# Attention stage of a hybrid decoder layer: three PSUM banks in turn for transposed probabilities, four for scores, with scores issued three tiles ahead instead of four

## What is computed

```python
s_win = jnp.einsum('bhqd,bkd->bhqk', qb, k_win).astype(f32) * scale
p_win = jax.nn.softmax(jnp.where(m_win, s_win, NEG_INF), axis=-1).astype(v_win.dtype)
o_win = jnp.einsum('bhqk,bkd->bhqd', p_win, v_win)
```

## Time and profile before

| | |
|---|---|
| median of three runs | 603.61 us (603.17 to 603.81) |
| the profiled execution | 603.88 us, of which the span is 602.1 us |
| PE busy | 590.5 us (98% of the span) |
| DVE busy | 390.1 us (65%) |
| ACT busy | 300.0 us (50%) |
| POOL busy | 257.0 us (43%) |
| attention loop | about 156.7 to 210 us of the span |
| granted TensorE clock | 0.997 of full speed |

### The profile page before, as it was taken

How to read it: one execution, slowest core, us unless ns; L and a number is a source line. 1 busy time by engine, 2 the same in 40 slices (tenths; PEclk the granted TensorE clock), 3 DMA queues, 4 the chain that set the end, 5 groups by cost and what they waited for, 6 DMA issues and landing times.

```text
span 602.1 us, 8286 instructions
## 1 busy us (share of the span) xinstructions
PE 590.5 (98%) x3095; PEld 484.5 (80%) x3095; DVE 390.1 (65%) x666; ACT 300.0 (50%) x529; POOL 257.0 (43%) x138
## 2 busy tenths in 40 slices
PE   8999999999999999999999999999999999999995
PEld 5898888877866678899878888888888888888884
DVE  6414605266978774983999777585595685771656
ACT  6713414654589934555645545444355265354322
POOL 7763323573094610043357443631723626611611
PEclk9999999999999999999999999999999999999998
DMA  8743282466023710028034340621603404104002
GB/s 326 288 144 137 72 208 71 87 161 208 1 45 104 264 63 0 1 72 280 1 143 137 136 144 1 209 71 67 202 12 139 141 0 153 57 1 175 1 35 106
DMA packets 36580, 67.18 MB, mean 112 GB/s; under 512 B 2876, under 2 KB 23612, under 8 KB 35516
## 3 DMA queue, kind: packets, MB, share of 16 engines
q1 hardware_dynamic: 36236, 66.25, 34.0%
q10 hardware_dynamic: 304, 0.39, 0.3%
HBM read 62.18 MB, written 2.10 MB: 107 GB/s over the span
## 4 chain that ended last, share of the span: by engine, by line
PE 89%; ACT 4%; DVE 3%; issue 2%; DMA 1%; SPq 0%; POOLq 0%; POOL 0%; ACTq 0%; DVEq 0%
PE ps L1814 19%; PE ps L1816 19%; PE ps L1815 19%; PE ps L2288 7%; PE ps L2290 7%; PE ps L2289 7%; PE ps L2140 2%; PE ps L2155 2%; PE ps L2051 1%; PE ps L2052 1%; ACT probs L949 1%; DMA x_land<-in_x_turned 1%; ACT W L890 1%; PE ps L1979 1%; PE ps L2216 1%
## 5 line engine op out<-in xcount | busy, mean ns | idle before, releaser
L1814 PE MATMUL ps<-xT_h,ring_h 128*128 128x512 f32 (+1 forms) x384 | 144.3, 376 | 0.3 <-DVE q_far L1361 0.3
L1816 PE MATMUL ps<-xT_h,ring_l 128*128 128x512 f32 (+1 forms) x384 | 143.2, 373 | 0.0
L1815 PE MATMUL ps<-xT_l,ring_h 128*128 128x512 f32 (+1 forms) x384 | 143.1, 373 | 0.0
L773 POOL TENSOR_TENSOR ring_l<-raw_d,ring_h 128x1024 fp32r<-128x1024 f32 x25 | 67.3, 2699 | 129.8 <-ACT ring_h L1044 129.8
L773 POOL TENSOR_TENSOR ring_l<-raw,ring_h 128x1024 fp32r<-128x1024 f32 x31 | 76.7, 2499 | 77.5 <-DVE xres L1630 38.1
L692 POOL TENSOR_TENSOR ring_l<-raw,ring_h 128x512 fp32r<-128x512 f32 (+2 forms) x26 | 64.2, 2489 | 74.1 <-ACT ring_h L796 74.1
L1724 DVE TENSOR_TENSOR y<-ps,y 128x512 f32<-128x512 f32 x90 | 61.2, 689 | 50.9 <-PE ps L2290 50.6
L1814 PEld LDWEIGHTS ps<-xT_h,ring_h 128*128 128x128 f32 x384 | 72.4, 188 | 14.0 <-issue 1.3
L1816 PEld LDWEIGHTS ps<-xT_h,ring_l 128*128 128x128 f32 x384 | 72.3, 188 | 12.9
L1815 PEld LDWEIGHTS ps<-xT_l,ring_h 128*128 128x128 f32 x384 | 72.4, 189 | 12.5
L2288 PE MATMUL ps<-ring_h,a_h 128*128 128x512 f32 x196 | 76.7, 391 | 0.1
(11 more groups left out here) (276 smaller groups left out, 994.7 us busy)
## 6 DMA issues: line engine op xcount, KB each, us to landing
raw<-in_w_mlp SPq DMA_DIRECT2D x16, 1024.0 KB, 5.6
raw_d<-in_w_mlp SPq DMA_DIRECT2D x16, 1024.0 KB, 6.1
raw<-in_w_groups SPq DMA_DIRECT2D x8, 1024.0 KB, 4.8
xres<-in_x SPq DMA_DIRECT2D x8, 512.0 KB, 6.3
raw<-in_nsa_cmp_w SPq DMA_DIRECT2D x8, 512.0 KB, 6.6
raw<-in_w_groups SPq DMA_DIRECT2D x8, 256.0 KB, 5.5
raw<-in_w_out SPq DMA_DIRECT2D x2, 1024.0 KB, 6.2
raw<-in_w_out SPq DMA_DIRECT2D x4, 512.0 KB, 4.8
```

Of the source, the lines that this page charges most:

```text
L773: nc.gpsimd.tensor_tensor(slot(ring_l, n), slot_source(n), slot(ring_h, n).bitcast(F32), ALU.subtract).then_inc(lo_done, 1)
L1814: nc.tensor.matmul(o, sh, mh, start=start, stop=False)
L1815: nc.tensor.matmul(o, sh, ml, start=False, stop=False)
L1816: return nc.tensor.matmul(o, sl, mh, start=False, stop=stop)
```

## The change

Scores get four banks instead of five, and transposed probabilities three instead of two. The banks of the transposed probabilities are no longer tied to the head but taken in turn. So `transposes(s)` waits for the copy of tile s - 3 instead of s - 2 (a copy that the other engine makes), and `score(s)` waits for the exponential of tile s - 4 instead of s - 5. In PE's loop iteration s issues `score(s + 3)` instead of `score(s + 4)`; the waits for `cs_sub` and for `reads(J_MK[1])` move into iterations 0 and 2. On DVE `copy_t(u)` is ahead of `row_max(2u + 4)`. Behind the loop `y_transposes(2)` comes after `values(5)` and waits for `attn_out(4)`; it has bank 6 instead of 3.

```diff
-S_BANK = [2, 3, 7, 1, 0]
+S_BANK = [2, 3, 7, 1]
+T_BANK = [4, 5, 0]
-YT_BANK = [1, 2, 3, 2, 4, 5, 3, 2]
+YT_BANK = [3, 2, 6, 2, 4, 5, 3, 2]
@@ copy_t on ACT (L958), on DVE (L1510)
-ps[:, 5, 0:(i + 1) * P]
+ps[:, T_BANK[(2 * u + 1) % 3], 0:(i + 1) * P]
-ps[:, 4, 0:(i + 1) * P]
+ps[:, T_BANK[2 * u % 3], 0:(i + 1) * P]
@@ DVE's loop
                 if u + 1 < NU:
                     row_max(2 * u + 3)
+                copy_t(u)
                 if u + 2 < NU:
                     row_max(2 * u + 4)
-                copy_t(u)
@@ score(s); exp and row_max take S_BANK[s % 4] as well
-                if s >= 5:
-                    pe.wait_ge(p_ready, s - 4)
+                if s >= 4:
+                    pe.wait_ge(p_ready, s - 3)
-                bank = S_BANK[s % 5]
+                bank = S_BANK[s % 4]
@@ transposes(s)
-                if u >= 1:
-                    pe.wait_ge(pt_a if m else pt_v, u)
+                if s >= 3:
+                    pe.wait_ge(pt_v if m else pt_a, (s - 3) // 2 + 1)
-    nc.tensor.transpose(ps[:, 4 + m, ...
+    nc.tensor.transpose(ps[:, T_BANK[s % 3], ...
@@ PE's loop
-            pe.wait_ge(cs_sub, 1)
-            score(3)
-            pe.wait_ge(*reads(J_MK[1]))
...
+                    if s == 0:
+                        pe.wait_ge(cs_sub, 1)
+                    if s == 2:
+                        pe.wait_ge(*reads(J_MK[1]))
-                    if s + 4 < 2 * NU:
-                        score(s + 4)
+                    if s + 3 < 2 * NU:
+                        score(s + 3)
@@ behind the loop
+            values(last_pair)
+            pe.wait_ge(bt_used, last_pair)
             y_transposes(2)
-            values(last_pair)
```

More of the change, by code:

```diff
@@ L948, in exp @@
                     act.wait_ge(t_done, s - 2)
-                nc.scalar.activation(probs[:, s % 3, 0:w], ps[:, S_BANK[s % 5], 0:w], ACT.Exp,
+                nc.scalar.activation(probs[:, s % 3, 0:w], ps[:, S_BANK[s % 4], 0:w], ACT.Exp,
                                      bias=stat[:, NMAX + s:NMAX + s + 1],
@@ L958, in copy_t @@
                 nc.scalar.activation(block_of(pT[:, g % 2], 1, i, slice(0, i + 1)),
-                                     ps[:, 5, 0:(i + 1) * P].rearrange("p (j q) -> p j q", q=P), ACT.Copy).then_inc(pt_a, 1)
+                                     ps[:, T_BANK[(2 * u + 1) % 3], 0:(i + 1) * P].rearrange("p (j q) -> p j q", q=P), ACT.Copy).then_inc(pt_a, 1)
             def copy_o(g):
@@ L1466, in row_max @@
                 dve.wait_ge(s_done, s + 1)
-                nc.vector.tensor_reduce(stat[:, NMAX + s:NMAX + s + 1], ps[:, S_BANK[s % 5], 0:w], AX.X, ALU.max,
+                nc.vector.tensor_reduce(stat[:, NMAX + s:NMAX + s + 1], ps[:, S_BANK[s % 4], 0:w], AX.X, ALU.max,
                                         negate=True).then_inc(mx_done, 1)
@@ L1510, in copy_t @@
                 nc.vector.tensor_copy(block_of(pT[:, g % 2], 0, i, slice(0, i + 1)),
-                                      ps[:, 4, 0:(i + 1) * P].rearrange("p (j q) -> p j q", q=P)).then_inc(pt_v, 1)
+                                      ps[:, T_BANK[2 * u % 3], 0:(i + 1) * P].rearrange("p (j q) -> p j q", q=P)).then_inc(pt_v, 1)
             def coefficients(g):
@@ L2136, in transposes @@
                 pe.wait_ge(p_ready, s + 1)
-                if u >= 1:
-                    pe.wait_ge(pt_a if m else pt_v, u)
+                if s >= 3:
+                    pe.wait_ge(pt_v if m else pt_a, (s - 3) // 2 + 1)
                 for j in range(u % NT + 1):
-                    last = nc.tensor.transpose(ps[:, 4 + m, j * P:(j + 1) * P], probs[:, s % 3, j * P:(j + 1) * P], ident[:])
+                    last = nc.tensor.transpose(ps[:, T_BANK[s % 3], j * P:(j + 1) * P], probs[:, s % 3, j * P:(j + 1) * P], ident[:])
                 last.then_inc(t_done, 1)
```

## The result

The changed kernel takes 604.57 us (603.94 to 605.37, 19 runs) against 603.61 us (602.84 to 604.56, 19 runs): a ratio of 1.0017, with an interval of 1.001 to 1.0024. It is 1.0 us slower, forecast were 0.4. The profiled execution has a span of 602.7 us, 0.6 more than before; one execution of a kernel differs from the next by as much, so the trace is used for stretches within the attention loop and the medians for the whole.

The account below looks back on a forecast made before the run. PE, busy 98% of the span, was taken as the bound. Start -0.8, pairs +0.7 and +0.1, last pair 0.0, `y_transposes` +0.4 gave +0.4 us: a median of 604.0, range 602.3 to 605.9.

Parts of the forecast that it names:

- within 0.2%: Whole kernel: the time stays between 602.4 and 604.8 us; chance 0.58, against 0.15 for faster and 0.27 for slower.
- The start: Stretch before `values(0)`: 0.8 us less, 0.62 of it a displaced score and 0.2 gained.
- The pairs: Four pairs from `values(0)` to `values(4)`: 36.0 us against 35.30, +0.7, and 0.1 more for pair 2.
- The step from position 6 to `values`: In each pair, the chain through `attn_out` takes 3.14 us against PE's own 2.69, a new wait of 0.45.
- the term of `coefficients`: DVE's list in pairs 0 and 1: a small instruction takes 1.02 us, not 0.22, making the list late by 0.40.
- rival C: Position 6, behind `copy_o` on ACT: a lead of three is too short, PE waits for exponentials; 606.3 us, chance 0.20.
- The end: Stretch from `values(4)` to `values(5)`: laid out to 7.7 us, upper bound 8.3, with 0.0 in the sum.
- `y_transposes(2)`: Behind `values(5)`: its four transposes lose the cover of the wait for the last copy, +0.4 us.
- B: Attention loop: bank waits vanish, `attn_out` doesn't bind, nothing replaces them; pairs of 8.30 us, 601.1 in all, chance 0.14.
- D: Second instruction of `attn_out`, pair 0 or 1: interference with POOL, up to 1.2 us once; 604.6 to 605.2, chance 0.16.

Follow-up runs that it names:

- all_three: The changed kernel with `attn_out` ahead of the `row_max` of 256 columns, `coefficients` one query tile earlier and `y_transposes(2)` ahead of `values(5)`: 601.77 us, ratio 0.9965.

## Why the prediction was right, and where its sizes were off

The median was forecast at 604.0 and is 604.57, inside the range, on the side that was given; 1.0 us is near the bound of what is called a difference here, and of the three chances the one of "within 0.2%" (0.58) held.

**The start.** `values(0)` was to come 0.8 earlier. From PE's first score of the loop it was 10.74 before and is 10.00 now: -0.74. Right in size, and the wait for the projection's bank is gone, as the forecast said. That DVE's list sets the time of `values(0)` isn't shown: the second `cmp_gated` ended at 166.12, 0.05 ahead of it, but PE came to it without an idle time of its own, at the same 0.16 behind the score ahead of it as before. The two end together.

**The pairs.** +0.8 was forecast, +1.13 measured. The step from position 6 to `values` held: in pair 1 DVE's copy starts at 182.01 and `values` at 184.41, 2.40 later, forecast were 2.48.

```profile
182.01 0.68 DVE L1511 COPY pT<-ps 128x512 f32<-128x512 f32 x1
182.61 0.42 DVE L1468 TENSOR_REDUCE stat<-ps 128x1 f32<-128x256 f32 x1
182.94 0.68 DVE L1539 TENSOR_TENSOR work<-ps,stat 128x512 f32<-128x512 f32 x1
183.66 0.69 DVE L1540 TENSOR_TENSOR y<-y,work 128x512 f32<-128x512 f32 x1
```

The missing 0.08 is the last step: from the end of `attn_out` (184.35) to PE it is 0.06, where the forecast took the 0.14 that it had read between a copy and transposes. Before the change `attn_out` was therefore in time by 0.19, not 0.11.

What was mis-sized is the term of `coefficients`. I took its slow instruction as it stood in the trace: slow in pairs 0 and 1, 0.2 in pairs 2 and 3, plus 0.1. In the changed kernel it takes 0.93, 0.79, 0.80 and 0.72. So pair 3 is 9.35 instead of 8.95 (0.55 more on the list) and pair 2 is 8.84 instead of 8.75, while pair 1, at 0.79 instead of 1.02, is 8.84 instead of 9.15. The reasoning named this as the likeliest mistake, but gave a lucky 0.2 too much trust; the waits for a boundary of POOL's instructions are better taken at their mean. Its bound for this term was too small as well: by its own list, 1.3 in pairs 2 and 3 would cost 0.70 and 1.10, 1.8 us in all, and not "0.7 to 0.9 more".

Pair 0 is 9.40 instead of 9.15, since there ACT and not `attn_out` was last (the 0.55 at 174.36). That is rival C, in one pair, not by the mechanism that was laid out (`copy_o` ahead of position 6) but by the `moba_high` copy ahead of position 0, which the layout left out. The same holds for position 7 in pair 3: DVE's late list reaches PE by two ways, over the copies to `attn_out` and over the `row_max` to the exponential.

**The end.** From `values(4)` to `values(5)` 7.73 against a forecast 7.7, that is +0.05 where 0.0 was in the sum. `y_transposes(2)`: +0.44, as the trace of the run with it ahead showed (0.78 of idle time back to 0.34).

**Sum.** -0.74 + 1.13 + 0.05 + 0.44 = 0.88 in the trace, against 0.4.

**The rivals.** B (nothing takes the waits' place) is refuted by the waits for L1540, and what it asked for, pairs of 8.3, came true in pairs 1 to 3 once DVE was cleared (all_three). D was real but not last in the changed kernel; in three of the variants it was last in pair 0, by 0.13. The rule of the Trainium skill, "SBUF — State Buffer", "Who interferes with whom", that a VectorE instruction contends with GpSimd when it has two SBUF inputs and not when it has one, held where it was put to the test: the two-input form took 0.72 to 0.93 in the place in which the one-input form took 0.20 in all four pairs. That the blocking engine is POOL was argued from two ends that coincide (in the kernel before, 171.47 and 171.43); the 38 of 44 cases above and the four with POOL idle bear it out. No run left POOL's work out.

## What to carry to other kernels

When a wait for a buffer is removed, look up the next wait of the same consumer and by how much it was in time: here less than 0.2 us, and one small reduction put ahead of it was enough. In a queue that runs in order, put what others wait for ahead of what has slack, and put work that can be slow for reasons outside the engine where the engine stands idle anyway. Shortening a lead to pay for a buffer is a trade whose sides can be measured apart. And where an instruction's time depends on another engine's phase, read its duration in every trace before the effect of an edit is read from the total: here it once hid a gain of 0.33 us in two pairs and once a loss of the same size.

## What the runs showed of the hardware

In the kernel with the banks but not the lead, the clock of TensorE fell within the attention loop, which it does in none of the others. The windows of 2 us, columns as above, with the granted clock third from the end:

```profile
186.00:188.00 2.00, 0.21 (x3) 0.02 (x1) 1.89 (x5) 2.00 (x4) 0.29 (x1) 1.00 0.00 0
188.00:190.00 2.00, 1.93 (x7) 0.87 (x9) 0.69 (x1) 1.21 (x6) 2.00 (x2) 0.64 0.03 8
190.00:192.00 2.00, 2.00 (x10) 0.59 (x8) 0.00 (x0) 0.00 (x0) 2.00 (x3) 0.51 0.00 0
```

PE had been idle for 1.86 us when it resumed at 188.07, and from soon after that until about 192 it had half of its clock, the lower of its two levels (1.2 GHz); in the window from 192 to 194 the clock is 1.00 again. The 16 products of `values` took 3.85 us instead of 2.38. There are three such waits of 1.9 us; behind the first two the clock fell, so that they cost some 3.4 each, and behind the third, at 213.37, it did not (2.38 for `values`). What tells these apart is open, and there is only this one trace of it. Waits of up to 0.87 us, the longest in this loop in the other kernels, left the clock at 1.00. An idle time of PE is thus not always paid once.
